# Stick-breaking scores: the plain fp32 products replaced by pairs of rounded fp32 (fp32r) products

## The chip, the cores and the metric

The kernel runs on one core of a Trainium2 chip. The metric is the device time of one execution in microseconds (us). The kernel before took 1433.49 us, the median of three runs (1431.26 to 1433.74).

## The reference, cut to what matters

Two transformer blocks for 512 positions of width 1024. The first block has differential attention (4 heads), stick-breaking attention (8 heads of width 64) and a routed mixture of 32 experts. The second has latent attention, a Fourier mix and a gated feed-forward part. The change touches only the scores of the stick-breaking attention:

```
def stick_breaking(q, k, v):
    scale = q.shape[-1] ** -0.5                      # 1/8
    ...
        z = jnp.einsum('bhqd,bhkd->bhqk', qb, k).astype(jnp.float32) * scale
        log_1m = jnp.where(causal, jax.nn.log_sigmoid(-z), 0.0)
        between = lax.cumsum(log_1m, axis=3, reverse=True) - log_1m
        a = jnp.where(causal, jnp.exp(jax.nn.log_sigmoid(z) + between), 0.0)
```

## The kernel before, in words

Every engine has its own program and the programs meet at semaphores; the order on each engine is written out by hand. All products on TensorE (PE) go through the helper `mm` (L58), so most rows name L58 and are told apart by their tiles.

**Two sorts of product.** A product on plain fp32 tiles shows as two matmul records in the trace. A product on tiles of type fp32r (fp32 rounded for the fast path) shows as one record. To keep fp32 accuracy with fp32r, the kernel splits both operands into a high part (the value rounded to fp32r) and a low part (value minus high part) and adds three products: high by high, high by low, low by high (`three`, L67). The projections of the first block do that: weights UH and UL, normed input HH and HL.

**The projection stage** (about 17 to 122 us). A loop over n = 0 to 15. Per n, PE does 24 fp32r products of 512 columns (L706 to L738). ScalarE (ACT) makes the high weights of unit n+1 (`proj_high`, L1438), VectorE (DVE) the low ones (`proj_low`, L1971). n = 0 to 3 give the stick-breaking queries, n = 4 to 7 the keys, transposed (64 rows a head, two heads above each other on 128 rows), n = 8 to 11 the stick-breaking values, n = 12 to 15 the values of the other attention. At n = 1 to 4 ACT copies one query unit from PSUM to `sq`, times 1/8 (L1455). At n = 5 to 8 DVE copies one key unit to `sk` (L2044). In unit n = 8 PE waits for the four key copies in front of its fourth block k = 3 (L732).

**The score stage** (about 122 to 234 us). A loop over i = 0 to 9 (L776). For i < 8 PE makes the scores of head i: for each key tile c (128 keys) one plain fp32 product of 512, 384, 256 or 128 query columns, in the order c = 2, 3, 1, 0 (L784 to L786). Then for head i-1 it does the norm product (`head_norm`, L767, a plain fp32 product on all 128 rows) and the sums over keys (`below`, L750: LH, LL by TRI, and plain TMP by CST). Then comes `projection(i)` (L757), 24 fp32r products into bank 6, for the queries and keys of the other attention. At i = 3, 5, 7 and 9 the weights times values of two finished heads follow (64-column tiles). ACT takes the square for the norm (L1489), the logs of head i (L1468 to L1472) once the scores are there, the reciprocal root (L1403, L1406), and the exponentials of head i-1 (L1479). DVE adds max(z, 0) (L2060), GpSimd (POOL) masks (L598), DVE splits into LH and LL (L2063, L1971). DVE also writes the normed rows of the other attention (L1974, `dqk_out`), and `projection(i)` waits for the write of the round before (L761), since that write reads bank 6.

**Behind it.** The differential attention (to about 300 us), the output projection, the routing, the experts (about 373 to 820 us), and the second block. SyncE (SP) issues nearly all loads in a fixed order, each behind a wait for whatever used its place last.

The memory: `sq` and `sk` lie in B3. MORE is a block of 4096 columns that first holds an expert's weights, loaded behind the score stage.

Of the kernel before, what the change touches and what calls it, by code (L numbers as in the profile page):

```python
# [56 lines left out]
def mm(e, o, l, r, first, last):  # L57
    return e.matmul(o, l, r, start=first, stop=last, skip_group_check=True)  # L58
# [20 lines left out]
def body(nc, ctx, I, out):  # L79
# [11 lines left out]
    def sem(name):  # L91
        return ctx.enter_context(nc.semaphore(name))
# [73 lines left out]
    OHB = TMP[0:32, 3072:3712]  # L166
    brs = B3[0:4, 6144:6784]
    HH, HL = (again(n, [128, 8, 512], o) for n, o in (("HH", "B23"), ("HL", "TO")))
    dq, dk, sq, sk = (B3[:, 2048 * m:2048 * m + 2048].rearrange("p (m n) -> p m n", m=4) for m in range(4))
    dv = B1[:, 0:2048].rearrange("p (t n) -> p t n", t=4)  # L170
    sv = B1[:, 2048:4096].rearrange("p (t n) -> p t n", t=4)
    INIT = B1[0:64, 0:2 * NCOL].rearrange("p (n w) -> p n w", w=2)
# [217 lines left out]
    def slot(i, n, cols, at=0):  # L390
# [18 lines left out]
        sem(n) for n in ("eps_set", "zero_set", "x_rstd", "xn_act", "xn_dve", "qg_set", "brow_mm", "brow_cp"))  # L409
    xT_mm, hT_hi, hT_lo, proj_hi, proj_lo, proj_mm = (  # L410
        sem(n) for n in ("xT_mm", "hT_hi", "hT_lo", "proj_hi", "proj_lo", "proj_mm"))
    dn_act, dn_mm, dqk_out, dv_out, sq_out, sk_out, sv_out = (
        sem(n) for n in ("dn_act", "dn_mm", "dqk_out", "dv_out", "sq_out", "sk_out", "sv_out"))
    tb_set, lam_dot, lam_exp, lam_set, cs_exp, cs_set = (
        sem(n) for n in ("tb_set", "lam_dot", "lam_exp", "lam_set", "cs_exp", "cs_set"))
    da_r, da_q = sem("da_r"), sem("da_q")
# [21 lines left out]
        sem(n) for n in ("go_dve", "go_pe", "go_act", "ov_dve", "ov_pe", "ov_act", "ov_wa", "ov_wb", "ov_w2", "ov_step", "ov_done"))  # L438

    spent = x_in + [prm_in, cst_in, ohb_in, brow_out, tbr_in, zero_out, eps_set, x_rstd, x_sq, xs_act, xn_act, xn_dve, qg_set, brow_mm, brow_cp,  # L440
                    xT_mm, hT_hi, hT_lo, proj_hi, proj_lo, proj_mm, dn_act, dn_mm, dqk_out, dv_out, sq_out, sk_out, sv_out,
                    tb_set, lam_dot, lam_exp, lam_set, cs_exp, cs_set, da_s, da_max, da_exp, da_w, da_q, da_r, da_T, da_wt, da_o, od_out,
                    ada_mm, ada_row, ada_T, ada_mod, tri_set, sb_z, sb_log, sb_relu, sb_lsel, sb_split, sb_s, sb_exp,
                    sb_asel, sb_oT, sbn_act, sbn_mm, sbn_out, od_sq, od_rs, od_nrm, od_T, od_hi, od_lo, so_hi, so_lo, wo_hi, x1,
# [224 lines left out]
    def tensor(e):  # L669
# [31 lines left out]
        for n in range(16):  # L701
            kind, u = n // 4, n % 4
            hi, lo = UH[n % 2][:, :], UL[n % 2][:, :]
            if kind < 2:
                hi, lo = (w.rearrange("p (c n) -> p c n", c=8) for w in (hi, lo))
                if n == 6:  # L706
                    e.wait_ge(brow_cp, 2)
                if n == 7:
                    e.wait_ge(sq_out, 4)
                e.wait_ge(proj_lo, n + 1)  # L710
                for c in range(8):
                    if n == 0:
                        e.wait_ge(hT_lo, c + 1)
                    if c == 5 and n - 1 in ADA_AT:
                        ada_turn(ADA_AT[n - 1])
                    m = three(e, P[SK_BANKS[u] if kind else n], hi[:, c, :], lo[:, c, :], HH[:, c, :], HL[:, c, :], c == 0, c == 7)
                m.then_inc(proj_mm, 1)
                if n == 0:
                    e.wait_ge(ohb_in, 16)
                    e.wait_ge(prm_in, 16)  # L720
                    mm(e, P[6][0:4, :], RB, OHB[:, 0:512], True, True)
                    mm(e, P[7][0:4, 0:128], RB, OHB[:, 512:640], True, True).then_inc(brow_mm, 1)
            else:
                hi, lo = (w.rearrange("p (c n) -> p c n", c=2) for w in (hi, lo))
                if n == 8:
                    e.wait_ge(sq_out, 4)
                if n == 12:
                    e.wait_ge(sk_out, 4)
                e.wait_ge(proj_lo, n + 1)
                for k in range(4):  # L730
                    if k == 3 and n == 8:
                        e.wait_ge(sk_out, 4)  # L732
                    if k == 3 and n == 12:
                        e.wait_ge(sv_out, 4)
                    if k == 3 and n - 1 in ADA_AT:
                        ada_turn(ADA_AT[n - 1])
                    for c in range(2):
                        q = slice(128 * k, 128 * k + 128)  # L738
                        m = three(e, P[k if kind == 2 else DV_BANKS[k]], HH[:, 2 * u + c, q], HL[:, 2 * u + c, q], hi[:, c, :], lo[:, c, :],
                                  u == 0 and c == 0, u == 3 and c == 1)  # L740
                m.then_inc(proj_mm, 1)
            if n in ADA_AT:
                ada_product(ADA_AT[n])


        def place(i, c):
            lo = 256 if c == 3 else 0
            return P[3 * (i % 2) + min(c, 2)][:, lo:lo + 512 - 128 * c]
# [27 lines left out]
        for i in range(10):  # L776
            if i == 1:
                e.wait_ge(dv_out, 4)
            if i < 8:
                m, r = i // 2, slice(64 * (i % 2), 64 * (i % 2) + 64)  # L780
                for g in (2, 1, 0):
                    if i >= 2:
                        e.wait_ge(sb_exp, 3 * (i - 2) + 3 - g)
                    for c in blocks[g]:  # L784
                        t = mm(e, place(i, c), sk[r, m, 128 * c:128 * c + 128], sq[r, m, 128 * c:512], c < 3, True)
                    t.then_inc(sb_z, 1)  # L786
            if 1 <= i < 9:
                head_norm(i - 1)
                if i == 1:
                    e.wait_ge(tri_set, 1)  # L790
                for g in (2, 1, 0):
                    e.wait_ge(sb_split, 6 * (i - 1) + 2 * (3 - g))
                    for c in blocks[g]:
                        o = place(i - 1, c)
                        t = below(i - 1, o, ntri, ntr, c)
                        for d in range(c + 1, 4):
                            t = below(i - 1, o[:, 128 * (d - c):512 - 128 * c], none, nor, d)
                    t.then_inc(sb_s, 1)
            if i < 8:
                if i == 0:  # L800
                    e.wait_ge(dv_out, 4)
                projection(i)
            if i >= 3 and i % 2:
                m = (i - 3) // 2
                e.wait_ge(dn_act, 3 * min(i - 1, 7) + 2)
                if m:
                    e.wait_ge(sb_oT, m)
                e.wait_ge(sb_asel, 8 * m + 8)
                for c in range(4):
                    for j, x in enumerate((2 * m, 2 * m + 1)):  # L810
                        t = mm(e, P[7][64 * j:64 * j + 64, 128 * c:512], sv[:, c, 64 * x:64 * x + 64],
                               AE[x % 3][:, off[c]:off[c] + 512 - 128 * c], c == 0, c == 3)
                t.then_inc(sb_o, 1)
# [583 lines left out]
    def scalar(e):  # L1397
# [47 lines left out]
        for n in range(16):  # L1445
            if n == 1:
                e.wait_ge(zero_set, 2)
                e.dma_start(tdram.rearrange("(s n) w -> s (n w)", s=CAP), B1[0:64, 0:2 * NCOL]).then_inc(zero_out, 16)
                e.wait_ge(lam_dot, 2)
                e.activation(lt[:, 2:4], lt[:, 0:2], ACT.Exp).then_inc(lam_exp, 1)  # L1450
                e.activation(ce, cc, ACT.Exp, scale=-1.0).then_inc(cs_exp, 1)
            proj_high(n + 1)
            if 1 <= n <= 4:
                e.wait_ge(proj_mm, n)
                e.activation(sq[:, n - 1, :], P[n - 1], ACT.Copy, scale=0.125).then_inc(sq_out, 1)  # L1455
            if n == 12:
                e.wait_ge(proj_mm, 12)
                for k in range(4):
                    e.activation(sv[:, k, :], P[k], ACT.Copy).then_inc(sv_out, 1)
# [509 lines left out]
    def vector(e):  # L1969
        def minus(dst, src, high):  # L1970
            return e.tensor_tensor(dst, src, high, ALU.subtract)  # L1971
# [43 lines left out]
        for n in range(16):  # L2015
# [11 lines left out]
            if n == 1:  # L2027
                e.wait_ge(lam_exp, 1)
                e.tensor_tensor(nlam, lt[:, 3:4], lt[:, 2:3], ALU.subtract).then_inc(lam_set, 1)
                e.wait_ge(lam_set, 1)  # L2030
                e.tensor_scalar(nlam, nlam, -0.2, None, ALU.add).then_inc(lam_set, 1)
                e.tensor_scalar(slg, slg, 0.8, None, ALU.mult).then_inc(lam_set, 1)
                e.wait_ge(cs_exp, 1)
                step = Steps(e, cs_set)
                step(e.tensor_scalar(ce, ce, 1.0, None, ALU.add))
                step(e.reciprocal(ce, ce))
                step(e.memset(CS, 0.0))
                e.tensor_tensor(CS[:, :, 0:2], cc, ce, ALU.mult).then_inc(cs_set, 1)
                e.tensor_copy(TRI[:, :], CST[:, C_NTRI:C_NTRI + 256]).then_inc(tri_set, 1)
            if 5 <= n <= 8:  # L2040
                if n == 5:
                    e.wait_ge(brow_out, 16)
                e.wait_ge(proj_mm, n)
                e.tensor_copy(sk[:, n - 5, :], P[SK_BANKS[n - 5]]).then_inc(sk_out, 1)  # L2044
            if n - 1 in ADA_AT:
                ada_cols(ADA_AT[n - 1])
        e.wait_ge(zero_out, 16)
# [742 lines left out]
```

## Time and profile before

| | |
|---|---|
| median of three runs | 1433.49 us |
| the profiled execution | 1435.44 us, of which span 1433.7 us |
| PE busy | 1386.6 us (97%) |
| PE weight load (PEld) busy | 871.9 us (61%) |
| DVE, ACT, POOL busy | 619.8, 444.1, 59.3 us |
| chain that ended last | PE 86%, DMA 8%, DVE 3%, ACT 2% |
| granted TensorE clock | 0.996 on average |

The busy time of PE is from the first to the modelled end of its records. Matmuls are pipelined, so the pitch (from the start of one record to the start of the next) is what a product costs in a run of products, not its own duration. PEld is the load of the stationary operand, which can run beside a product.

### The profile page before, as it was taken

The numbers are of one execution on the slowest core, as the hardware profiler recorded it, in microseconds if no ns is written. First come the engines' busy times: TensorE is split into PE (matmuls) and PEld (weight loads), VectorE is DVE, ScalarE is ACT, GpSimd is POOL, SyncE is SP. The second block draws the span as 40 slices with busy tenths as digits, with TensorE's granted clock in tenths as the row PEclk, the third lists the DMA queues.
The fourth block names the chain that finished last, engine by engine and source line by source line (L and its number), as shares of the span: only waits on it lengthen the run. The fifth ranks groups of instructions, "written<-read, shape, count | busy, mean of one in ns | idle before, by whom it ended". The sixth has DMA issues, their size and how long they took to land.

```text
span 1433.7 us, 16158 instructions
## 1 busy us (share of the span) xinstructions
PE 1386.6 (97%) x6524; PEld 871.9 (61%) x6524; DVE 619.8 (43%) x1104; ACT 444.1 (31%) x755; POOL 59.3 (4%) x113
## 2 busy tenths in 40 slices
PE   6999999899999999999999999999999999999998
PEld 5777775576533333333333375655678888888886
DVE  5225555835434334433343465487353232233224
ACT  4124775623010010001200263386353222223232
POOL 0000110000210001001000001000000000000000
PEclk9999999899999999999999999999999999999999
DMA  8541117618899999999999923000053313313001
GB/s 350 219 170 59 59 60 294 264 59 333 320 424 425 424 423 424 424 428 425 421 424 427 374 74 147 1 1 1 0 235 117 118 59 117 117 59 118 30 0 59
DMA packets 32371, 304.07 MB, mean 212 GB/s; under 512 B 6315, under 2 KB 6315, under 8 KB 10536
## 3 DMA queue, kind: packets, MB, share of 16 engines
q1 hardware_dynamic: 29592, 298.69, 51.6%
q0 software_dynamic: 2272, 3.52, 0.7%
q8 instruction: 53, 0.87, 0.2%
q10 hardware_dynamic: 432, 0.81, 0.2%
q14 instruction: 22, 0.18, 0.0%
HBM read 302.59 MB, written 4.25 MB: 214 GB/s over the span
## 4 chain that ended last, share of the span: by engine, by line
PE 86%; DMA 8%; DVE 3%; ACT 2%; issue 1%; DVEq 0%; SPq 0%; POOL 0%; ACTq 0%
PE ps L58 81%; DMA ring<-in_w 7%; PE ps L1291 2%; PE ps L1011 1%; PE ps L967 1%; DMA MORE<-in_w_gu 1%; DMA X<-in_x 0%; PE ps L678 0%; PE ps L698 0%; PE ps L880 0%; ACT WH L1856 0%; PE ps L926 0%; ACT TO L1574 0%; DVE TMP L2190 0%; DVE TMP L1974 0%
## 5 line engine op out<-in xcount | busy, mean ns | idle before, releaser
L58 PE MATMUL ps<-ring,B 128*64 128x512 f32 (+3 forms) x624 | 146.8, 589 | 2.4 <-DMA ring<-in_w 1.2
L58 PE MATMUL ps<-XH,WH 128*128 128x512 f32 (+1 forms) x368 | 140.6, 382 | 1.3 <-DVE XL L1971 0.7
L58 PE MATMUL ps<-XL,WH 128*128 128x512 f32 (+1 forms) x368 | 139.8, 380 | 0.0
L58 PE MATMUL ps<-XH,WL 128*128 128x512 f32 (+1 forms) x368 | 139.7, 380 | 0.0
L1633 ACT ACTIVATE TMP<-ps 64x512 f32<-64x512 f32 x32 | 19.0, 594 | 302.7 <-PE ps L58 301.6
L58 PE MATMUL ps<-B 128*64 128x512 f32 (+5 forms) x408 | 110.2, 555 | 0.3 <-DMA B<-in_w 0.3
L2307 DVE TENSOR_TENSOR X<-ps,X 128x512 f32<-128x512 f32 x112 | 72.2, 686 | 63.7 <-PE ps L58 63.7
L58 PEld LDWEIGHTS ps<-ring,B 128*64 128x64 f32 (+1 forms) x624 | 43.7, 137 | 78.0 <-issue 73.8
L1856 ACT ACTIVATE WH<-ring 128x2048 fp32r<-128x2048 f32 x24 | 46.0, 1918 | 126.3 <-PE ps L58 126.3
L1971 DVE TENSOR_TENSOR WL<-ring,WH 128x2048 fp32r<-128x2048 f32 x24 | 55.0, 2292 | 66.2 <-ACT WH L1856 66.2
L58 PE MATMUL ps<-ring,TMP 128*64 128x512 f32 x336 | 75.3, 594 | 5.0 <-DMA ring<-in_w 5.0
L58 PEld LDWEIGHTS ps<-XH,WH 128*128 128x128 f32 x368 | 69.1, 188 | 16.0 <-DVE XL L1971 1.9
L58 PEld LDWEIGHTS ps<-XL,WH 128*128 128x128 f32 x368 | 69.2, 188 | 13.2
L58 PEld LDWEIGHTS ps<-XH,WL 128*128 128x128 f32 x368 | 69.2, 188 | 13.2
L2630 DVE TENSOR_TENSOR B<-ps,TMP 128x512 f32<-128x512 f32 x22 | 15.2, 692 | 134.4 <-PE ps L58 134.4
L58 PE MATMUL ps<-WH,XH 128*128 128x512 f32 x176 | 68.5, 389 | 0.0
L58 PE MATMUL ps<-WL,XH 128*128 128x512 f32 x176 | 68.5, 389 | 0.0
L58 PE MATMUL ps<-WH,XL 128*128 128x512 f32 x176 | 68.5, 389 | 0.0
L1971 DVE TENSOR_TENSOR UL<-ring,UH 128x1024 fp32r<-128x1024 f32 x32 | 39.1, 1223 | 61.1 <-ACT UH L1438 46.0
L58 PE MATMUL ps<-B,TMP 128*64 128x512 f32 (+4 forms) x264 | 52.4, 432 | 7.5 <-ACT TMP L1562 5.1
L1974 DVE SCALAR_TENSOR_TENSOR YL<-ps,MISC,YH 128x512 fp32r<-128x512 f32 x32 | 24.0, 750 | 79.4 <-ACT YH L1617 79.4
L58 PEld LDWEIGHTS ps<-B 128*64 128x64 f32 (+2 forms) x408 | 36.7, 154 | 35.4 <-issue 31.3
(365 smaller groups left out, 2442.5 us busy)
## 6 DMA issues: line engine op xcount, KB each, us to landing
ring<-in_w SPq DMA_DIRECT2D x57, 2048.0 KB, 26.9
B<-in_w SPq DMA_DIRECT2D x21, 2048.0 KB, 27.8
ring<-in_w_ada SPq DMA_DIRECT2D x12, 2048.0 KB, 8.4
MORE<-in_w SPq DMA_DIRECT2D x11, 2048.0 KB, 25.4
ring<-in_w_gu SPq DMA_DIRECT2D x8, 2048.0 KB, 8.0
TO<-in_w SPq DMA_DIRECT2D x7, 2048.0 KB, 18.9
ring<-in_w_in SPq DMA_DIRECT2D x6, 2048.0 KB, 12.2
ring<-in_w_down SPq DMA_DIRECT2D x4, 2048.0 KB, 7.3
```

Of the source, the lines that this page charges most:

```text
L58: return e.matmul(o, l, r, start=first, stop=last, skip_group_check=True)
L967: t = e.transpose(P[n][:, 128 * q:128 * q + 128], XG[:, 128 * c:128 * c + 128], ident)
L1011: t = e.transpose(P[5 if x == NE - 1 else 4][:, 64 * f:64 * f + 64], HG[x % 2][:, 128 * f:128 * f + 128], ident[0:64, 0:64])
L1291: t = e.transpose(o[:, 128 * c:128 * c + 128], E2[y % 3][:, 128 * c:128 * c + 128], ident)
L1633: e.activation(SL, P[2 + x % 2][64:128, :], ACT.Silu).then_inc(up_sl, 1)
L1856: e.activation(WH[n % 2][:, :].rearrange("p (c n) -> p c n", c=src.shape[1]), src, ACT.Copy).then_inc(ws_hi, 1)
L1971: return e.tensor_tensor(dst, src, high, ALU.subtract)
L1974: return e.scalar_tensor_tensor(out=dst, in0=src, scalar=s, in1=other, op0=ALU.mult, op1=op1)
L2307: e.tensor_tensor(xs, P[h if k % 2 else 6 + h], xs, ALU.add).then_inc(cm_add, 1)
L2630: e.tensor_tensor(aT[:, f, :], P[(2 * f + 4) % 8 + 1 if f else 1], SG[f % 2], ALU.mult).then_inc(at_dve, 1)
```

## The change

A unit of keys or queries holds two heads, head j on rows 64j to 64j+63. `sq` and `sk` go. For each key unit there is now a KS tile with two planes: plane j holds the high part of head j's keys on that head's own 64 rows and their low part on the other 64 rows. For each query unit QS has two planes as well: plane j holds the high part of head j's queries on both halves. QL holds the low part of the queries on their own rows.

A score tile is then two fp32r products: KS by QS over all 128 rows (high by high plus low by high), and the high half of KS by QL over 64 rows (high by low). The tile c = 3, which has 128 query columns, is widened to 256 columns: its own and the 128 before them, read in exchanged order; the second half of the result lies in unused columns of the bank. Each head so has eight products on 512, 384, 256 and 256 columns, alternately with 128 and with 64 rows.

The parts are made in the projection stage. ACT writes four half tiles for a query unit (n = 1 to 4) in place of one copy, and two high half tiles for a key unit (n = 5 to 8). DVE writes two low half tiles for a query unit (new) and two for a key unit (in place of one copy). QS 2 and 3 and QL lie in MORE, the others in B3. PE's waits follow: L709 waits for the queries' parts, L726 and L728 go, L732 waits for all parts.

```diff
+                for to in (0, 1):
+                    for j in range(2):
+                        r, d = slice(64 * j, 64 * j + 64), slice(64 * (j ^ to), 64 * (j ^ to) + 64)
+                        e.activation(QS[n - 1][d, j, :], P[n - 1][r, :], ACT.Copy, scale=0.125).then_inc(s_high, 1)
-                e.activation(sq[:, n - 1, :], P[n - 1], ACT.Copy, scale=0.125).then_inc(sq_out, 1)
+            if 5 <= n <= 8:                                   # ACT
+                e.wait_ge(proj_mm, n)
+                for j in range(2):
+                    r = slice(64 * j, 64 * j + 64)
+                    e.activation(KS[n - 5][r, j, :], P[SK_BANKS[n - 5]][r, :], ACT.Copy).then_inc(s_high, 1)
...
+            if 1 <= n <= 4:                                   # DVE
+                e.wait_ge(s_high, 4 * n)
+                for j in range(2):
+                    r = slice(64 * j, 64 * j + 64)
+                    times(QL[r, n - 1, :], P[n - 1][r, :], 0.125, QS[n - 1][r, j, :], ALU.subtract).then_inc(s_low, 1)
             if 5 <= n <= 8:
-                if n == 5:
-                    e.wait_ge(brow_out, 16)
-                e.wait_ge(proj_mm, n)
-                e.tensor_copy(sk[:, n - 5, :], P[SK_BANKS[n - 5]]).then_inc(sk_out, 1)
+                e.wait_ge(s_high, 2 * n + 8)
+                for j in range(2):
+                    r, d = slice(64 * j, 64 * j + 64), slice(64 - 64 * j, 128 - 64 * j)
+                    minus(KS[n - 5][d, j, :], P[SK_BANKS[n - 5]][r, :], KS[n - 5][r, j, :]).then_inc(s_low, 1)
...
                     for c in blocks[g]:                       # PE
-                        t = mm(e, place(i, c), sk[r, m, 128 * c:128 * c + 128], sq[r, m, 128 * c:512], c < 3, True)
+                        ks, o = KS[m][:, i % 2, 128 * c:128 * c + 128], place(i, c)
+                        qs, ql = QS[m][:, i % 2, 128 * c:512], QL[:, m, 128 * c:512]
+                        if c == 3:
+                            o = P[3 * (i % 2) + 2][:, 256:512].rearrange("p (a n) -> p a n", a=2)
+                            qs = QS[m][:, i % 2, 256:512].rearrange("p (a n) -> p a n", a=2)[:, ::-1, :]
+                            ql = QL[:, m, 256:512].rearrange("p (a n) -> p a n", a=2)[:, ::-1, :]
+                        mm(e, o, ks, qs, c < 3, False)
+                        t = mm(e, o, ks[r], ql[r], False, True)
                     t.then_inc(sb_z, 1)
```

## Rows read from the trace of the kernel before

**Rows 1.** The page: busy time, share of the span and count of each engine.
```profile
PE 1386.6 (97%) x6524; PEld 871.9 (61%) x6524; DVE 619.8 (43%) x1104; ACT 444.1 (31%) x755; POOL 59.3 (4%) x113
```

**Rows 2.** Chain of waits, 112 to 235 us: start us, us, what.
```profile
124.70 94.24 PE ps L58 x450
```

**Rows 3.** Waits of PE, 122 to 218 us: us in total, times, longest.
```profile
PE ps L58 <- DVE B L2050: 0.3, 1, 0.3
```

**Rows 4.** Timeline, head 2's scores in and out: start, us, engine, line, rows*columns of weights.
```profile
141.72 0.39 PE L58 MATMUL ps<-HH,UL 128*128 128x512 f32 x1
142.04 0.48 PE L58 MATMUL ps<-B 64*128 64x256 f32 x1
142.36 0.19 PEld L58 LDWEIGHTS ps<-B 64*128 64x128 f32 x1
142.57 0.71 PE L58 MATMUL ps<-B 64*128 64x128 f32 x3
...
143.44 1.02 PE L58 MATMUL ps<-B 64*128 64x512 f32 x2
143.87 0.59 PE L58 MATMUL ps<-B 64*128 64x512 f32 x1
144.39 0.30 PEld L58 LDWEIGHTS ps<-ring,CST 128*128 128x128 f32 x2 [0.76 <-issue]
...
144.92 0.59 PE L58 MATMUL ps<-ring,CST 128*128 128x512 f32 x1
```

**Rows 5.** Timeline, an fp32r product, then plain transposes (L698) behind a wait in the program.
```profile
87.44 0.39 PE L58 MATMUL ps<-UH,HL 128*128 128x512 f32 x1
...
87.68 0.60 PE L698 MATMUL ps<-CST,TMP 128*128 128x128 f32 x4
```

**Rows 6.** Timeline, pitches of fp32r products: 384 columns, 512, 256.
```profile
134.56 0.34 PE L58 MATMUL ps<-LL,TRI 128*128 128x384 f32 x1
134.74 0.28 PE L58 MATMUL ps<-LH,TRI 128*128 128x256 f32 x1
...
141.49 0.39 PE L58 MATMUL ps<-HL,UH 128*128 128x512 f32 x1
...
1062.27 0.28 PE L58 MATMUL ps<-XH,WH 128*128 128x256 f32 x1
1062.39 0.28 PE L58 MATMUL ps<-XL,WH 128*128 128x256 f32 x1
```

**Rows 7.** Timeline, values' products of two heads, then scores of head 4.
```profile
167.43 0.27 PE L58 MATMUL ps<-ring,B 128*64 128x128 f32 x1
167.63 0.29 PEld L58 LDWEIGHTS ps<-B 64*128 64x128 f32 x2 [0.17 <-issue]
```

**Rows 8.** Timeline, round 2: max on DVE, normed write, load of the next projection.
```profile
144.68 0.56 DVE L2060 SCALAR_TENSOR_TENSOR TMP<-ps,TMP 128x384 f32<-128x384 f32 x1 [1.89 <-ACT TMP L1472]
...
147.00 0.75 DVE L1974 SCALAR_TENSOR_TENSOR B<-ps,PRM,LW 128x512 f32<-128x512 f32 x1 [0.36 <-ACT LW L1406]
...
148.01 0.19 PEld L58 LDWEIGHTS ps<-HH,UH 128*128 128x128 f32 x1
```

**Rows 9.** Timeline around unit n = 8; the last is its block k = 3's first load.
```profile
70.79 1.06 ACT L1438 ACTIVATE UH<-ring 128x1024 fp32r<-128x1024 f32 x1 [6.93 <-PE ps L58]
73.02 0.68 DVE L2044 COPY B<-ps 128x512 f32<-128x512 f32 x1
74.45 0.19 PEld L58 LDWEIGHTS ps<-UH,HH 128*128 128x128 f32 x1
```

**Rows 10.** Timeline of SP: loads behind the score stage, then the experts' stream.
```profile
227.21 0.81 SPq L512 DMA_DIRECT2D ring<-in_w_ada  x2
...
364.29 0.34 SPq L512 DMA_DIRECT2D MORE<-in_w  x1
```

**Rows 11.** Windows: us, busy (x) of PE, PEld, DVE, ACT, POOL, clock, DMA share, GB/s.
```profile
122.00:218.00 96.00, 95.71 (x451) 69.75 (x452) 54.31 (x92) 67.13 (x122) 16.27 (x60) 1.00 0.12 45
...
350.00:365.00 15.00, 15.00 (x94) 9.91 (x94) 8.14 (x32) 0.31 (x2) 0.00 (x0) 1.00 0.67 257
```

More of the change, by code:

```diff
@@ L168, in body @@
     HH, HL = (again(n, [128, 8, 512], o) for n, o in (("HH", "B23"), ("HL", "TO")))
-    dq, dk, sq, sk = (B3[:, 2048 * m:2048 * m + 2048].rearrange("p (m n) -> p m n", m=4) for m in range(4))
+    dq, dk = (B3[:, 2048 * m:2048 * m + 2048].rearrange("p (m n) -> p m n", m=4) for m in range(2))
+    KS = [again(f"KS{m}", [128, 2, 512], "B23", 8192 + 1024 * m) for m in range(4)]
+    QS = [again(f"QS{m}", [128, 2, 512], "B23" if m < 2 else "MORE", 6144 + 1024 * m if m < 2 else 1024 * m - 2048) for m in range(4)]
+    QL = again("QL", [128, 4, 512], "MORE", 2048)
     dv = B1[:, 0:2048].rearrange("p (t n) -> p t n", t=4)
@@ L411, in body @@
         sem(n) for n in ("xT_mm", "hT_hi", "hT_lo", "proj_hi", "proj_lo", "proj_mm"))
-    dn_act, dn_mm, dqk_out, dv_out, sq_out, sk_out, sv_out = (
-        sem(n) for n in ("dn_act", "dn_mm", "dqk_out", "dv_out", "sq_out", "sk_out", "sv_out"))
+    dn_act, dn_mm, dqk_out, dv_out, s_high, s_low, sv_out = (
+        sem(n) for n in ("dn_act", "dn_mm", "dqk_out", "dv_out", "s_high", "s_low", "sv_out"))
     tb_set, lam_dot, lam_exp, lam_set, cs_exp, cs_set = (
@@ L440, in body @@
     spent = x_in + [prm_in, cst_in, ohb_in, brow_out, tbr_in, zero_out, eps_set, x_rstd, x_sq, xs_act, xn_act, xn_dve, qg_set, brow_mm, brow_cp,
-                    xT_mm, hT_hi, hT_lo, proj_hi, proj_lo, proj_mm, dn_act, dn_mm, dqk_out, dv_out, sq_out, sk_out, sv_out,
+                    xT_mm, hT_hi, hT_lo, proj_hi, proj_lo, proj_mm, dn_act, dn_mm, dqk_out, dv_out, s_high, s_low, sv_out,
                     tb_set, lam_dot, lam_exp, lam_set, cs_exp, cs_set, da_s, da_max, da_exp, da_w, da_q, da_r, da_T, da_wt, da_o, od_out,
@@ L708, in tensor @@
                 if n == 7:
-                    e.wait_ge(sq_out, 4)
+                    e.wait_ge(s_high, 16)
+                    e.wait_ge(s_low, 8)
                 e.wait_ge(proj_lo, n + 1)
@@ L724, in tensor @@
                 hi, lo = (w.rearrange("p (c n) -> p c n", c=2) for w in (hi, lo))
[L725 to L728, printed above, removed]
                 e.wait_ge(proj_lo, n + 1)
@@ L731, in tensor @@
                     if k == 3 and n == 8:
-                        e.wait_ge(sk_out, 4)
+                        e.wait_ge(s_high, 24)
+                        e.wait_ge(s_low, 16)
                     if k == 3 and n == 12:
```

## The prediction

> **What bounds the kernel now.** I read the page first, then the chain of waits and PE's waits over the stage that changes, then the windows, and last the timeline of one round. The page [rows 1] shows PE busy for 97% of the span. From 124.70 us the chain [rows 2] runs 94.24 us on PE alone, so in the score stage every microsecond of PE counts. The waits [rows 3] say the same: between 122 and 218 us PE waits once, for 0.3 us, in round 0, where `projection(0)` waits for the four value copies of DVE. The windows [rows 11] have PE busy 95.71 of 96 us there, ACT 67.13 and DVE 54.31, at a granted clock of 1.00, the level of 2.4 GHz. So what the change is worth is read from PE's order, round by round.
>
> **What a head's scores cost now.** In round 2 [rows 4] the last projection product starts at 141.72. The pitch of such products is 0.23 (141.49 [rows 6] to 141.72), so it makes room at 141.95. The scores' first record starts at 142.04 and the next at 142.36, 0.32 later, while a record of the same size has a pitch of 0.21 (142.36 to 142.57). Entering the scores costs 0.09 of gap and 0.11 of a first load that nothing hides: 0.20. At the other end the last score record starts at 143.87 and has a pitch of 0.43 (143.44 to 143.87), so it makes room at 144.30. The norm's load starts at 144.39 and its second record at 144.92, 0.53 later where 0.43 is the pitch: again 0.09 plus 0.10, 0.19. With both ends the scores take from 141.95 to 144.92 - 0.43 = 144.49, or 2.54 us.
>
> What are these two 0.2 us? Neither a semaphore nor the change of type: in [rows 5] a plain product follows an fp32r one, with a wait of the program in between, and the pitch is 0.24, 0.01 above the usual. What differs in [rows 4] is the number of rows of the stationary tile: 128, then 64, then 128. PE seems to run empty and to load in the open whenever that shape changes. [Rows 7] show it for another pair of shapes: the last values' record starts at 167.43, its 128 columns have a pitch of 0.11 (half of the 256's 0.21), and the scores' load comes at 167.63, again 0.09 late.
>
> **What they cost after.** The streams get shorter. An fp32r product of 512 columns has a pitch of 0.227, one of 384 0.18, one of 256 0.12, even with new weights each time [rows 6]. A head has two of 512, two of 384 and four of 256 (the widened tile among them): 2 x (0.227 + 0.18 + 0.12 + 0.12) = 1.29 us. But the eight products have 128 and 64 rows by turns, and the norm behind the last has 128 again. That makes seven changes of shape inside and one on the way out; the way in has none, since projections and KS both have 128 rows. No row of before has a change between two fp32r products, so I bound its price. The lower end is 0, if it belonged to plain products only. The upper end is 0.28: the gap of 0.09 and the whole recorded load of 0.19 [rows 4]. I take 0.195, the mean of the two ends in [rows 4], the nearest rows: one of them has an fp32r product at one side, the other has none, and they cost the same. 8 x 0.195 = 1.56, and the head comes to 1.29 + 1.56 = 2.85 us against 2.54: 0.31 us more.
>
> **A rule beside it.** The Trainium skill, TensorEngine Tiling (Array Packing), section Key Properties, says that a change of the tiling mode, as opposed to a change of the tile alone, drains TensorE. By this rule, which makes no difference between types, the six added changes are all paid; without it a price of plain products only could stand, and the sum would be the first rival's. That two fp32r products with 128 and 64 rows pay it is shown by no row here.
>
> **Which rounds count.** Round 0: the scores' first record would start at 121.9 and PE then waits for DVE until 124.70 [rows 2]. 121.9 + 2.85, less the way out's load of 0.1, is 124.65, inside the wait: 0. Rounds 1 to 7 count 0.31 each, 2.2 us. In rounds 4 and 6 the values' products, with 64 columns of weights, stand in front of the scores: a change now [rows 7] and a change after, so there the way in is not saved, and 2 x 0.2 = 0.4 comes on top. Together 2.6 us.
>
> **The projection stage.** ACT gets three more half tiles for a query unit and two for a key unit. Its weights' copy of 1024 columns takes 1.06 [rows 9], so 0.53 for 512 columns; half the rows save nothing. In a unit it then does 1.06 + 4 x 0.53 = 3.2 us beside 24 x 0.227 = 5.44 of PE: hidden. DVE gets two writes of at most 0.75 each (the longest of 512 columns, [rows 8]): hidden too. One place is close. In unit n = 8 PE needs all key parts before its fourth block, whose first load is at 74.45 [rows 9]. ACT's high halves would end near 70.79 + 1.06 + 2 x 0.53 = 72.9. DVE comes free at 73.02, where the copy starts now, and two subtractions of 0.68 or a little more end at 74.4 to 74.5 in place of 73.70. I put 0.1 us on the path, once (0 to 0.3). Where the cover is gone, each further 0.1 of DVE counts whole.
>
> **What moves with it.** The logs of head i start when the c = 2 and 3 products are done, some 0.2 later than now, and the max (144.68, [rows 8]) with them. The normed write (147.00 to 147.75) and the projection's load (148.01) follow the norm on PE and move by the same 0.3. So nothing new is late in the score stage. No load is added and none changes its place in a queue. Later stages keep their distance: SP issues the load at 227.21 [rows 10] behind a wait for the stage's last products, and that of 364.29, with which the experts' stream begins, behind a wait for PE, after a window in which the DMA share was 0.67 [rows 11], so that stream had not begun to bind. A shift passes through whole.
>
> **The sum.** +2.6 +0.1 = +2.7 us. For the profiled execution the span goes from 1433.7 to 1436.4, its time from 1435.44 to 1438.1. It lies 1.95 above the median of the runs shown; for the median I predict 1433.5 + 2.7 = 1436.2 us, 0.19% more.
>
> **The rivals.** First, and on the other side: changes of shape between fp32r products are free. Place: the inside of each head. The head takes 1.29 and the norm comes 1.25 us earlier. Then the normed write gets late. The logs can begin about 0.35 earlier (the square for the norm holds them), so the max comes at 144.33 in place of 144.68, and the split behind it leaves DVE free for the write near 146.2 in place of 147.00, too late by 0.25 for the norm's gain: `projection` starts 1.0 earlier. 7 x 1.0 = 7.0: 1426.5 us, 0.5% faster. For it speaks that fp32r takes one record a product; against it that in [rows 4] the way in, behind an fp32r product, costs as much as the way out. It decides the sign from where a change costs under (2.54 - 1.29) / 8 = 0.16 us.
>
> Second, only the load is in the open, since running empty overlaps short streams: 1.29 + 8 x 0.11 = 2.17, 0.37 less a head, 2.6 in seven rounds, 0.2 back in rounds 4 and 6: 1431.1 us. [Rows 4] speak against it, for both ends there have the gap.
>
> Third, a change costs 0.28 between short products. 1.29 + 2.24 = 3.53, 0.99 more a head: 6.9 in seven rounds, 0.6 in rounds 4 and 6, 0.7 from round 0, which comes out of its cover, and 0.3 from the key parts: 1442.0 us, 0.6% slower. For it there is only the length of the load's record; against it that 0.11 of it was open at both ends of [rows 4].
>
> **How the numbers follow.** Forecast 0.72, with its own range of 1434.8 to 1437.8 (0.18 to 0.21 us for a change, and the scatter of the runs, the lowest 2.2 below the median). First rival 0.12, second 0.07, third 0.09. A measurement of this kernel can tell about 0.2% (2.9 us) from no change, and the forecast lies just within: I put 0.42 of it past 2.9, or 0.30. With the third that makes 0.39 for slower. The other 0.42 and 0.04 of the second make 0.46 for the same; 0.12 and 0.03 make 0.15 for faster. The range leaves out the first rival, part of the second and the far part of the third: 1432.0 to 1439.5 us.
>
> **What would show it.** In round 2 of the trace after: eight score records with pitches of about 0.31 (256 columns), 0.37 and 0.42, each load at the start of its own product and not beside the one in front, and 2.85 us from the projection's end to the norm's stream. If the pitches are 0.12 and 0.23, the first rival holds, and PE should wait for DVE L1974 in front of the projections. In unit n = 8 a wait of PE for DVE of up to 0.3 would show the close place. What would make the prediction wrong: a price of a change away from 0.2, or a shift that is not there any more at the loads of 227.21 and 364.29.

## The result and the profile after

The changed kernel took 1435.92 us (median of 21 runs, 1434.35 to 1438.1); the kernel before took 1433.74 us (21 runs, 1430.49 to 1435.22). The ratio is 1.0019, with a 95% interval of 1.0013 to 1.0025. The medians stand 2.2 us apart, the ratio means 2.7, and its interval 1.9 to 3.6; the 2.9 that I had called the border of a measurable change lies inside it. The forecast was 1436.2, 0.3 too high. The profiled execution took 1435.27 us, its span 1433.5, at a mean granted clock of 0.997.

The page of the kernel after: busy time, share of the span and count of each engine (it answers to [rows 1]).

```profile
PE 1387.4 (97%) x6524; PEld 872.0 (61%) x6524; DVE 629.1 (44%) x1116; ACT 456.1 (32%) x775; POOL 59.1 (4%) x113
```

DVE has 12 writes more and ACT 20, and neither shows in the time: the bound is PE, as before. The busy time of PE hardly moved (1386.6 to 1387.4) and is no measure of the change. From 122 to 218 us PE counts as busy for 96.00 us of 96 (95.71 before), so what it spends on the changes of shape is not seen as idle time. And this execution needed less elsewhere: 76.23 us in place of 77.30 between 246 and 332 us, a stretch that comes up again below.

The chain of waits of the kernel after, from 112 us on (start us, us, what; it answers to [rows 2]).

```profile
114.91 106.20 PE ps L58 x488
```

Before, the chain came onto PE at 124.70, where `projection(0)` starts behind DVE's value copies, and stayed there to 124.70 + 94.24 = 218.94. Now it is on PE without a break from 114.91 to 221.11.

`projection(0)` starts at 124.38 (its row is in the next fence), so the stage from there takes 221.11 - 124.38 = 96.73 us in place of 94.24: 2.49 us more, where 2.6 was forecast. I use this length for all kernels below, because the start of the stage itself lies up to 1 us earlier or later from one execution to the next.

Timeline of PE, round 0, in the kernel after: the last score record and `projection(0)`.

```profile
123.88 0.50 PE L58 MATMUL ps<-QL,KS 64*128 64x512 f32 x1
124.38 0.50 PE L58 MATMUL ps<-HH,UH 128*128 128x512 f32 x1
```

Timeline of round 2 of the kernel after, head 2's scores in and out, then the max, the normed write and the next projection's load (start, us, engine, line, rows*columns of weights; it answers to [rows 4, 8]).

```profile
141.94 0.28 PE L58 MATMUL ps<-QS,KS 128*128 128x256 f32 x1
142.14 0.18 PEld L58 LDWEIGHTS ps<-QL,KS 64*128 64x128 f32 x1 [0.24 <-issue]
142.14 0.38 PE L58 MATMUL ps<-QL,KS 64*128 64x256 f32 x1
...
142.46 0.38 PE L58 MATMUL ps<-QS,KS 128*128 128x256 f32 x1
...
143.08 0.44 PE L58 MATMUL ps<-QS,KS 128*128 128x384 f32 x1
...
143.45 0.44 PE L58 MATMUL ps<-QL,KS 64*128 64x384 f32 x1
...
143.82 0.49 PE L58 MATMUL ps<-QS,KS 128*128 128x512 f32 x1
...
144.24 0.50 PE L58 MATMUL ps<-QL,KS 64*128 64x512 f32 x1
...
144.88 0.56 DVE L2081 SCALAR_TENSOR_TENSOR TMP<-ps,TMP 128x384 f32<-128x384 f32 x1 [2.10 <-ACT TMP L1488]
...
145.24 0.68 PE L58 MATMUL ps<-LH,TRI 128*128 128x256 f32 x1
...
147.28 0.75 DVE L1990 SCALAR_TENSOR_TENSOR B<-ps,PRM,LW 128x512 f32<-128x512 f32 x1 [0.45 <-ACT LW L1414]
...
148.29 0.19 PEld L58 LDWEIGHTS ps<-HH,UH 128*128 128x128 f32 x1
```

Read the distances. The first record comes where the projection makes room (141.94), so the way in is free. It stands 0.20 before the second: 0.12 for its 256 columns and a gap of 0.09. From there on every record stands 0.31 (256 columns), 0.37 (384) or 0.42 (512) before the next, since it also holds the open load of its own tile: the load starts together with its product (142.14 and 142.14) and not beside the one in front. A stream of 256 columns alone needs 0.12. A head ends where the norm's second record starts less 0.43; in all these kernels I take the start of the LH row less 0.03 for that record (in the kernel before the two stand at 144.95 and 144.92), and 0.43 less for the end. Here 145.24 - 0.46 = 144.78, less 141.94: 2.84 us, against 2.54 before.

### The profile page after: what moved, and what is told of

The parts are those of the page before. It is cut to its first block, busy times and chain, and to the rows that moved or that the text cites. A ratio compares the mean times of both kernels' runs of the same rounds, so it can differ in the third digit from the quotient of the medians.

```text
span 1433.5 us, 16188 instructions
## 1 busy us (share of the span) xinstructions
PE 1387.4 (97%) x6524; PEld 872.0 (61%) x6524; DVE 629.1 (44%) x1116; ACT 456.1 (32%) x775; POOL 59.1 (4%) x113
## 4 chain that ended last, share of the span: by engine, by line
PE 88%; DMA 6%; DVE 3%; ACT 2%; issue 1%; DVEq 0%; SPq 0%; POOL 0%; ACTq 0%
PE ps L58 83%; DMA ring<-in_w 5%; PE ps L1299 2%; PE ps L975 1%; PE ps L1019 1%; DMA MORE<-in_w_gu 1%; DMA X<-in_x 0%; PE ps L681 0%; PE ps L701 0%; PE ps L888 0%; ACT WH L1872 0%; PE ps L934 0%; DVE TMP L1990 0%; DVE TMP L2211 0%; DVE X L2614 0%
## 5 line engine op out<-in xcount | busy, mean ns | idle before, releaser
L58 PE MATMUL ps<-B 128*64 128x512 f32 (+5 forms) x344 | 90.6, 575 | 0.2 <-DMA B<-in_w 0.2
L2351 DVE TENSOR_TENSOR TMP<-ps,TMP 64x512 f32<-64x512 f32 x32 | 21.8, 682 | 83.3 <-ACT TMP L1649 83.3
```

What stands on the lines that cost most here:

```text
L2351: e.tensor_tensor(HG[x % 2], P[2 + x % 2][0:64, :], SL, ALU.mult).then_inc(up_hg, 1)
```

## The experiments

Each kernel stands against the kernel before on the same chip, with its ratio. "The stage" is PE's piece of the chain from `projection(0)` to its end, 94.24 us before and 96.73 after. It comes from one profile each and is what I read; the timed differences have a scatter of their own and stand up to 1.6 us away from it, as the table shows.

| kernel | stage, us less than before | medians, us less than before |
|---|---|---|
| both products on 128 rows | 6.67 | 5.5 |
| both on 64 rows | 5.95 | 5.7 |
| grouped by shape | 2.75 | 4.3 |
| 128 rows, write ahead | 8.46 | 8.4 |
| plain products on 128 rows | 2.31 | 3.9 |
| narrow tile not widened | 8.53 | 9.6 |
| key parts ahead | 8.46 | 9.9 |

### Both products on all 128 rows

```diff
-                        t = mm(e, o, ks[r], ql[r], False, True)
+                        t = mm(e, o, ks, ql, False, True)
```

The second product runs over all 128 rows, so it adds the other head's low keys by low queries, a term as small as the one that the split leaves out anyway. Columns, count and buffers stay; only the changes of shape go.

> Changed kernel, but the second product of a score tile uses all 128 rows of KS and QL as well. It so adds the low keys of the head times the low queries of the other head of the pair, a term of the size of the low by low product that is left out anyway. Streams, writes and columns stay as they are; only the change from 128 to 64 rows and back is gone. Theory A (each change of the stationary tile's shape costs 0.2 us): a head's scores fall from 2.84 to 1.29 us, with pitches of 0.12, 0.12, 0.12, 0.12, 0.18, 0.18, 0.23, 0.23; PE then waits in front of the projections for DVE's normed write, about 0.25 a round; rounds get 1.0 us shorter than in the kernel before: 7 us under the kernel before. Rival B (the price lies in the fp32r products themselves or in the widened tile, not in the shape): pitches stay at 0.31 to 0.42 and the time stays 2 us above the kernel before.

Measured: 1427.87 us (1425.0 to 1428.42), ratio 0.9962 (0.9949 to 0.9975) against 1433.33. The chain, then the timeline of round 2 of this kernel:

```profile
123.70 87.57 PE ps L58 x450
```

```profile
139.90 0.28 PE L58 MATMUL ps<-QS,KS 128*128 128x256 f32 x1
139.91 0.19 PEld L58 LDWEIGHTS ps<-QL,KS 128*128 128x128 f32 x1
140.01 0.28 PE L58 MATMUL ps<-QL,KS 128*128 128x256 f32 x1
...
141.65 0.68 PE L58 MATMUL ps<-LH,TRI 128*128 128x256 f32 x1
...
144.16 0.74 DVE L1990 SCALAR_TENSOR_TENSOR B<-ps,PRM,LW 128x512 f32<-128x512 f32 x1
...
144.60 0.38 PE L58 MATMUL ps<-TMP,CST 128*128 128x128 f32 x2
144.95 0.19 PEld L58 LDWEIGHTS ps<-HH,UH 128*128 128x128 f32 x1 [0.17 <-DVE B L1990]
```

The load of the second product now starts at 139.91, beside the first (139.90 to 140.18), and the pitch of 256 columns is 0.11. The head takes 141.65 - 0.46 - 139.90 = 1.29 us, to the hundredth the sum of streams in the prediction. So this kernel is the world of the first rival, and its second half shows too: DVE's normed write ends at 144.90 and the projection's load, due 0.11 behind 144.60, waits for it until 144.95, 0.24 late (0.25 was worked out). The stage is 94.24 - 87.57 = 6.67 us shorter than before; the rival had 7.0. The rival's sum leaves a term out: in rounds 4 and 6 the way in still costs a change, from the values' tiles with 64 columns, and 7.0 less 0.4 is 6.6.

### Both products on 64 rows

```diff
-                        mm(e, o, ks, qs, c < 3, False)
+                        mm(e, o, ks[r], qs[r], c < 3, False)
```

This leaves out the product of low keys by high queries.

> Changed kernel, but the first product of a score tile uses only the head's own 64 rows, so both have 64 rows. It leaves out the low keys times the high queries. Theory A: two changes of shape a head in place of eight, 1.29 + 2 x 0.195 = 1.68 us against 2.54 before, so 0.86 less in rounds 1 to 7: 6 us under the kernel before. Rival C (a product on 64 rows of fp32r is itself slow, whatever stands in front of it): eight such products cost at least what four do in the changed kernel, 2 us or more above the kernel before.

Measured: 1427.59 us (1425.58 to 1429.77), ratio 0.9964 (0.995 to 0.9978) against 1433.33. The chain and the timeline of round 2:

```profile
124.18 88.29 PE ps L58 x450
```

```profile
140.31 0.39 PE L58 MATMUL ps<-HH,UL 128*128 128x512 f32 x1
140.63 0.38 PE L58 MATMUL ps<-QS,KS 64*128 64x256 f32 x1
140.85 0.28 PE L58 MATMUL ps<-QL,KS 64*128 64x256 f32 x1
140.97 0.28 PE L58 MATMUL ps<-QS,KS 64*128 64x256 f32 x1
...
142.67 0.68 PE L58 MATMUL ps<-LH,TRI 128*128 128x256 f32 x1
```

With 64 rows throughout, inner pitches are 0.12 again (140.85 to 140.97), so the price does not belong to 64 rows as such. It stands at the two ends: the first record comes 0.32 behind the projection's last and leads the next by 0.22. The head takes from 140.31 + 0.23 = 140.54 to 142.67 - 0.46 = 142.21, 1.67 us: 1.29 and two changes of 0.19. The stage is 5.95 us shorter than before.

### The same products, grouped by shape

```diff
+                for part in (0, 1):
                     for g in (2, 1, 0):
...
+                            if part == 0:
+                                mm(e, o, ks, qs, c < 3, False)
+                            else:
+                                t = mm(e, o, ks[r], ql[r], False, True)
```

The arithmetic is that of the change; a head's four products of 128 rows come first, then its four of 64 rows.

> Changed kernel with the same eight products a head in another order: the four with 128 rows first, then the four with 64 rows. Theory A: two changes a head (one in, one out) in place of eight: 1.68 us. The scores for the logs come later than in the all-128 version (about 1.1 us after the start), so DVE's chain in front of the normed write holds the projections: rounds about 0.5 us shorter than before, 3.5 us under the kernel before (2 to 6). Rivals B and C: no difference to the changed kernel, 2 us above the kernel before.

Measured: 1428.99 us (1428.08 to 1429.81), ratio 0.9971 (0.9959 to 0.9982) against 1433.33. The timeline of round 2:

```profile
140.73 0.81 PE L58 MATMUL ps<-QS,KS 128*128 128x256 f32 x4
141.46 0.91 PE L58 MATMUL ps<-QL,KS 64*128 64x256 f32 x4
...
142.87 0.68 PE L58 MATMUL ps<-LH,TRI 128*128 128x256 f32 x1
...
145.81 0.38 PE L58 MATMUL ps<-TMP,CST 128*128 128x128 f32 x2
146.36 0.50 PE L58 MATMUL ps<-HH,UH 128*128 128x512 f32 x1 [0.16 <-DVE B L1994]
```

Two changes of shape in place of eight: 142.87 - 0.46 - 140.73 = 1.68 us a head. By PE alone the stage should be 7 x 0.86 less 0.4 (one change more than before in rounds 4 and 6), 5.6 us, shorter than before. It is 2.75 shorter (its pieces of the chain run from 124.01 to 215.50, 91.49 us), because c = 2 and 3 are finished only near the end of the head. The logs of ACT start later, the max of DVE behind them too, and the normed write, which stands behind the max, is late for the projection: its first load is due 0.11 behind 145.81 and comes with the product at 146.36, 0.44 late. The chain runs over this write in seven rounds, 7 x 0.44 = 3.1 us. PE has its gain and gives about half of it to DVE.

### All 128 rows, with the normed write ahead on DVE

Both products stand on 128 rows here too; the lines are DVE's.

```diff
                 for g in (2, 1, 0):
...
+                    if g == 2 and i >= 1:
+                        normed_write(i - 1)          # directly behind the first max
-                if g == 2 and 1 <= i <= 8:
-                    ...                              # was behind the first split
```

> As the version with all 128 rows, but DVE does the normed write (dqk_out) directly behind the first max of the round, in front of the split that waits for POOL. Theory A with the wait of the first rival: the wait of PE for DVE in front of the projections goes, rounds are 1.25 us shorter than before, 8.7 us under the kernel before, 1.7 less than the version without the new order. If that wait is not there or another one takes its place (the split of g = 2 comes later, the norm itself waits): same time as that version within 0.5 us.

Measured: 1424.89 us (1423.64 to 1427.12), ratio 0.9942 (0.993 to 0.9955) against 1433.33. The chain, then the write on DVE and the projection's load:

```profile
123.93 85.78 PE ps L58 x450
```

```profile
143.68 0.75 DVE L1990 SCALAR_TENSOR_TENSOR B<-ps,PRM,LW 128x512 f32<-128x512 f32 x1 [0.85 <-ACT LW L1414]
...
144.69 0.19 PEld L58 LDWEIGHTS ps<-HH,UH 128*128 128x128 f32 x1
```

The write ends at 144.43, and the load at 144.69 shows no wait. The stage is 8.46 us shorter than before (7 x 1.25 less the 0.4 of rounds 4 and 6 would be 8.35; the expected 8.7 left that 0.4 out), 1.79 of it from DVE's order: the seven waits of about 0.25 us that the faster PE had run into. This version beats both kernels, by 0.6% the kernel before.

### The kernel before, its plain products on 128 rows

```diff
-                        t = mm(e, place(i, c), sk[r, m, 128 * c:128 * c + 128], sq[r, m, 128 * c:512], c < 3, True)
+                        t = mm(e, place(i, c), sk[:, m, 128 * c:128 * c + 128], sq[:, m, 128 * c:512], c < 3, True)
```

Every score so sums over both heads of the pair and is not the reference's.

> The kernel before, with its plain fp32 score products over all 128 rows in place of 64: each score then sums over both heads of the pair, so the scores are not the reference's; the columns and the count of products stay. The two changes of shape at the ends of a head's scores go; the streams are the same. Theory A (a change between 128-row and 64-row stationary tiles costs 0.2 us, whatever the type): a head takes 2.15 us in place of 2.54, 0.39 less in seven rounds; in rounds 4 and 6 the values' products with 64 columns stand in front, so one change of the two stays there. 7 x 0.39 - 2 x 0.2 = 2.3 us less than before: 1431.0. Round 0 stays hidden. Theory B (the 0.2 us at each end belong to a new group of products or to a type, not to the number of rows): the two gaps of 0.2 us stay in the trace and the time is that of before within 0.3 us. The scores have other values, so if the routing changed with them the later stages would differ; then only the score stage of the trace is read (97.3 us before; A: 95.0, B: 97.3).

Measured: 1430.07 us (ten runs, 1428.4 to 1430.7), ratio 0.9972 (0.9962 to 0.9981) against 1433.99. The chain and the timeline of PE around head 2:

```profile
124.21 91.93 PE ps L58 x450
```

```profile
140.82 0.39 PE L58 MATMUL ps<-HH,UL 128*128 128x512 f32 x1
141.05 2.32 PE L58 MATMUL ps<-B 128*128 128x256 f32 x8
...
143.66 0.68 PE L58 MATMUL ps<-LH,TRI 128*128 128x256 f32 x1
```

The plain product now follows the fp32r one at the usual pitch of 0.23 (140.82 to 141.05), where [rows 4] had 0.32 and an open load. The head takes 143.66 - 0.46 - 141.05 = 2.15 us, 0.39 less than 2.54, and the stage 94.24 - 91.93 = 2.31 us less, as worked out from 0.195 (2.3). What I had read as "entering and leaving the scores" is the number of rows, in plain fp32 too. The timed difference, 3.9 us between the medians, is larger than the stage's 2.31; the part on the granted clock below shows where such a rest can come from. Since the scores have other values, the work behind the routing may differ as well, and I read the stage alone.

### The narrow tile not widened

```diff
-                        if c == 3:
+                        if False:
```

The rest is the version of all 128 rows with the write ahead.

> As e4_write_first (both products on all 128 rows, the normed write first on DVE), with the tile c = 3 on its own 128 query columns, not widened to 256. Theory A (the fp32r stream of 128 columns is shorter than that of 256 or at worst as long, bound by the load of about 0.11 us): the two narrow products have pitches of 0.11 us at most 0.12, a head is 1.29 us or up to 0.05 shorter, and the time that of e4_write_first within 0.5 us: 1424.9. Theory B (fp32r runs slower per column in narrow products, the reason for the widening): pitches of 0.2 to 0.23 us for the narrow products, 0.2 us more a head, seven rounds: +1.4 us, 1426.3.

Measured: 1424.38 us (1423.47 to 1425.8), ratio 0.9936 (0.9923 to 0.995) against 1433.99. PE's timeline of head 2:

```profile
140.13 0.22 PE L58 MATMUL ps<-QS,KS 128*128 128x128 f32 x1
140.19 0.28 PE L58 MATMUL ps<-QL,KS 128*128 128x128 f32 x1
140.31 0.39 PE L58 MATMUL ps<-QS,KS 128*128 128x384 f32 x1
140.53 0.34 PE L58 MATMUL ps<-QL,KS 128*128 128x384 f32 x1
```

From the first narrow record to the second one of 384 columns it is 0.40 us; the widened form needs 0.12 + 0.12 + 0.18 = 0.42. PE's piece of the chain is 85.71 us, 0.07 less than in the widened form. The short stream (0.06) is followed by longer distances (0.12, and 0.22 where 384 columns alone take 0.18). The loads around it start at 140.13, 140.24 and 140.35, 0.11 apart, so here it is the loads that set the pace. So theory A's time holds, though not by equal pitches. The widening neither costs nor brings anything measurable here.

### The key parts ahead of the weights' parts in unit 8

```diff
+            if n != 8:
                 proj_high(n + 1)        # ACT; the same with proj_low on DVE
...
+            if n == 8:
+                proj_high(n + 1)        # behind the keys' parts
```

The rest again is the version of all 128 rows with the write ahead.

> As e4_write_first, with one more move in unit n = 8 of the projection stage: ACT makes the keys' high parts ahead of the next unit's high weights, DVE the keys' low parts ahead of the next unit's low weights. Theory A (in the changed kernel PE waits 0.22 us for the key parts in front of the fourth block of unit 8): the wait goes, 0.2 us less: 1424.7, below what the times can tell; the fourth block's first load is at 73.98 in the trace, or 9 products of 0.227 us behind the block before, with no gap. Rival: the weights' parts of unit 9 get late by the move, and PE waits in front of unit 9 (about 75.5 us) by up to 1 us: 1425.9.

Measured: 1424.1 us (1423.6 to 1425.6), ratio 0.9937 (0.9923 to 0.995) against 1433.99. First unit 8 of the changed kernel, then of this one:

```profile
71.41 1.22 ACT L1471 ACTIVATE KS<-ps 64x512 fp32r<-64x512 f32 x2
...
72.67 1.41 DVE L1987 TENSOR_TENSOR KS<-ps,KS 64x512 fp32r<-64x512 f32 x2
...
73.98 0.39 PE L58 MATMUL ps<-UH,HL 128*128 128x512 f32 x1
74.19 0.19 PEld L58 LDWEIGHTS ps<-UH,HH 128*128 128x128 f32 x1 [0.25 <-issue]
74.22 0.47 PE L58 MATMUL ps<-UH,HH 128*128 128x512 f32 x1
...
74.53 0.40 PE L58 MATMUL ps<-UL,HH 128*128 128x512 f32 x1
```

```profile
70.84 1.41 DVE L1990 TENSOR_TENSOR KS<-ps,KS 64x512 fp32r<-64x512 f32 x2 [2.92 <-ACT KS L1472]
...
73.25 0.19 PEld L58 LDWEIGHTS ps<-UH,HH 128*128 128x128 f32 x1
73.48 0.19 PEld L58 LDWEIGHTS ps<-UL,HH 128*128 128x128 f32 x1
```

In the changed kernel the key parts are done at 72.67 + 1.41 = 74.08, and the load due at about 73.98 starts at 74.19. The stream loses less, since a load normally runs one product ahead: 74.22 to 74.53 is 0.31 in place of 0.23, with 0.02 around it, 0.1 us in all. With the key parts ahead the loads stand 0.23 apart throughout, from unit 8 into unit 9, and the rival's late weights do not come. The gain is below what the times can tell, as said.

## Why the prediction was right

**The price of a change of shape.** This was the step on which the sign hung, taken from two places with plain products and carried over to fp32r. The runs give it four times, each as a difference of heads in which only the rows of the stationary tiles or the order of the products differ:

| scores of a head | changes of shape | us | us for a change |
|---|---|---|---|
| fp32r, all 128 rows | 0 | 1.29 | |
| fp32r, all 64 rows | 2 | 1.67 | 0.19 |
| fp32r, grouped by shape | 2 | 1.68 | 0.195 |
| fp32r, alternating (the change) | 8 | 2.84 | 0.194 |
| plain, 128 rows | 0 | 2.15 | |
| plain, 64 rows (before) | 2 | 2.54 | 0.195 |

It is one price, for both types, in both directions, and for products of 256 to 512 columns alike (the pitches of 0.31, 0.37 and 0.42 are the streams of 0.12, 0.18 and 0.23 and this price). The first rival (0) and the third (0.28) are refuted by the change itself, the second (only the load, 0.11) as well. The rule of the Trainium skill, TensorEngine Tiling (Array Packing), section Key Properties, that a change of tiling mode drains TensorE, agrees with these rows; it gives no price.

**The stage.** 0.31 us in seven rounds and 0.4 in rounds 4 and 6 were 2.6; the stage grew by 2.49 (with the measured 0.30 a head it is 2.1 and 0.4, 2.5). Round 0 was hidden, but with nothing over: before, `projection(0)` waited 0.3 us for DVE [rows 3]; after, the score record of 123.88, its 0.42 and the gap of 0.09 lead to 124.38 or 124.39, where `projection(0)` starts, and DVE's copies end at 124.33. In the two kernels with all 128 rows (write behind and write ahead) that cover shows as a wait of 1.4 us for the value copies, which is why their gain counts in seven rounds and not eight. The max moved from 144.68 to 144.88, by the 0.2 forecast, the normed write and the projection's load by 0.28, and no wait for them came up.

**The projection stage.** The term was 0.1 us. The load is 0.2 late and the stream loses 0.1. DVE needed 1.41 us for two half tiles, 0.70 each, within the bound of 0.75; ACT 0.61 each where I had 0.53. ACT's added half tiles are hidden: between 17 and 122 us PE waits once for a semaphore that the profile names (0.9 us, for HL; 0.7 before).

**The shift behind it.** SP's load of the bias rows, behind a wait on PE, then two of the kernel after that answer to [rows 10], the second being the first of the experts' stream:

```profile
218.82 1.75 SPq L532 DMA_DIRECT2D TO<-biasrow  x4
...
229.38 11.07 SPq L515 DMA_DIRECT2D ring<-in_w_ada  x4
...
365.20 0.34 SPq L515 DMA_DIRECT2D MORE<-in_w  x1
```

Before, the first of them was at 216.64: 2.18 later now, of which the stage explains 2.49 less the 0.32 by which this execution reached the stage earlier. The load of 227.21 is at 229.38, 2.17 later, as forecast. At 365.20 only 0.91 are left against [rows 10], and the profiled execution as a whole came out at 1435.27 us, where 1438.1 was worked out, with a span within 0.2 us of the one before. Read by these two profiles alone, the claim "a shift passes through whole" would look wrong. The windows 246 to 332 us show where 1.3 us of it are; first the kernel before, then before with its plain products on 128 rows (the changed kernel has 0.98 there):

```profile
246.00:332.00 86.00, 77.30 (x398) 56.18 (x399) 49.24 (x159) 39.28 (x106) 0.00 (x0) 0.94 0.47 184
```

```profile
246.00:332.00 86.00, 75.41 (x417) 55.55 (x417) 51.52 (x162) 41.63 (x110) 0.00 (x0) 1.00 0.48 185
```

The column behind POOL is the granted clock: 0.94, 0.98 and 1.00 in a stretch in which the three kernels issue the same instructions; a mean below 1.00 says that for part of it only the lower of the two levels, 1.2 GHz, was granted. In windows of 4 us two such places show in the kernel before, around 270 us (0.69 from 270 to 274) and at 278 to 286 us (0.66, then 0.50 for the whole of 282 to 286, with PE busy throughout on 12 records); the changed kernel has the first alone (0.62 from 270 to 274). From the bias rows to the load of `in_w` into B behind this stretch SP's issues are 124.2 us apart before, 122.9 in the changed kernel and 121.3 in the third. The other six profiles fall on the same three values: 121.3 where the clock is 1.00 (three kernels), 122.8 at 0.98 (one, with the first low place alone), 124.2 at 0.94 (two, with both). So one execution can lose up to 2.9 us here that another doesn't, whatever the kernel. The profile before had lost it all, the profile after 1.6 of it; the difference of 1.3 hides more than half of the shift. The remaining 1.1 go in two parts, 0.8 between 697 and 822 us, among the last loads of the experts, and 0.3 up to 1080. No run shows the cause. But from the load of `in_w` into B (340.81 us in the kernel before) to the end of the span the nine profiles need 1091.8 to 1093.9 us (1092.9 before, 1091.8 after), so a difference of this size comes without any change of the score stage. That the shift arrives at the end is therefore not seen in the profiles but in the timed runs: over 21 each, the ratio gives 2.7 us, 1.9 to 3.6, and the sum with the measured terms is 2.49 + 0.1 = 2.6. That the rest of the difference in the plain kernel's times comes from this too is likely (its ten timed runs all had a mean clock of 0.998 or more, while 6 of the 14 runs of before beside them were below), but not shown.

**The chances.** The most likely case came. Its time lay almost on the border between "the same" and "slower", which had 0.46 and 0.39: the measured 2.7 us fall 0.2 short of it, and on which side of it they fell was luck.

## What to carry to other kernels

Where PE is the bound, look at the rows of the stationary tiles and not only at columns and types: in this kernel every step between 128 and 64 rows cost 0.195 us, more than a whole fp32r stream of 384 columns (0.18). Padding the short product with data whose sum does no harm (here low by low, all 128 rows) costs nothing in columns and gave back 1.55 us a head; grouping the products by shape gave 1.16, but delayed the first results, and DVE's write then came 0.44 too late for PE. And when PE gets faster, look at once for the engine that now comes late behind it: moving one write on DVE was worth 1.8 of the 8.5 us.

## What the runs showed of the hardware that was not expected

- fp32r products of 64 rows are not cheaper and not dearer than those of 128: 0.12 us for 256 columns in both (all 64 rows and all 128 rows).
- A load beside a running product of the same shape is hidden down to a pitch of 0.11 to 0.12 us, though its own record says 0.19. Below that it shows: after a stream of 128 columns (0.06) the loads stand 0.11 apart, and the distances of the products grow to 0.12 and 0.22.
- The granted clock of a busy stretch (246 to 332 us) differs from one execution to another, 0.94 to 1.00, with 2.9 us between the ends: up to two short places at the level of 1.2 GHz, the rest at 2.4 (0.50 from 282 to 286 us in the kernel before).
